# A hybrid decoder layer in fp32 halves: another order of the projections on all five engines

## The chip, the cores and the metric

One core of a Trainium2 chip runs the whole layer as one program. The metric is device time in microseconds (us), the median of several executions. TensorE (PE) does the matmuls, VectorE (DVE), ScalarE (ACT) and GpSimd (POOL) the element work, and SyncE (SP) issues every DMA. Each engine works through its own list in order; they meet only at semaphores.

## The reference, cut to what matters

```
c_act = silu(c);  mod = c_act @ w_ada + b_ada          # sh1, sc1, g1, sh2, sc2, g2: 1024 each
h    = rms_norm(x, norm1_g) * (1 + sc1) + sh1          # x: 2048 x 1024
proj = h @ w_in                                        # 1024 -> 2304: q,k,v | val,gate | bg,cg,xc | ud
ya   = diff_attention(q, k, v)                         # q, k rms-normed per 32 columns, causal
yb   = silu(layer_norm(causal_dwconv31(val * sigmoid(gate)) + b))     # 256 channels
yc   = bg * causal_dwconv3(cg * xc)
yd   = (pooled windows 2,4,8,16 of ud - ud) @ pool_w * pool_scale
x    = x + g1 * (concat(ya, yb, yc, yd) @ w_out)
x    = x + g2 * (relu(rms_norm(x)*(1 + sc2) + sh2 @ w_ff1)^2 @ w_ff2)
```

## The kernel before, in words

The program has three stages: the projections (to about 570 us), the attention (to about 950 us), and w_out with the MLP (the rest). Only the first is touched. Every fp32 operand of a projection is split into a rounded head (`h_hi`, `w_hi`, made on ACT) and a tail (`h_lo`, `w_lo`, made on DVE), and each product is three matmuls (lines L1617 to L1619). A weight item (256 columns) therefore goes SP load -> ACT head (L778) -> DVE tail (L1170), through one raw buffer: the next load waits for the tail.

The tokens come in two halves, h = 0 and 1, of 1024 each. A half has two parts.

*Row tiles*, t = 0 to 7, n = 8h + t. PE transposes a tile of x (`transposes`, L1627) into the first two PSUM banks; ACT applies gain and shift (`modulate`, eight instructions, L794) and makes the head (`h_head`, L800); DVE makes the tail (`h_tail`, L1165); then PE projects q, k and v of the tile. Before it is transposed, x is loaded by SP (`load_x`, two buffers), its mean square is taken by DVE (`mean_square`, L1149 to L1152), the root by ACT (`rms_root`, L785), and the rows are scaled by DVE (`normalise`, L1158 and L1159). In the kernel before, round t of the loops does the mean square, root and scaling of tile n+2 and the modulation, head and tail of tile n+1. q and k are normed by `qk_square`, `qk_sums`, `qk_normalise` (DVE, L1229 to L1239) and by POOL (`norm_gain`), and stored.

*Columns*: kinds gate, val, ud, cg, pool, xc, bg, each with two blocks of 512 tokens times two groups of 128 channels. The outputs go round a ring of six PSUM banks, and `free(o)` makes PE wait for the reader of the output six before. DVE multiplies val by the sigmoid of the gate into `conf` and then runs the 31-tap convolution: 124 instructions per half (`conv_taps`, L1256 and L1259), which other work calls for in portions by `pump(taps, n)`; what is left of them runs into the next half's row tiles, or into the attention. POOL sums the windows of ud (`windows`, L694 to L699) into `win_a` and `win_b`; DVE makes `pool_in` (`pooled`, L1294 to L1303); ACT may overwrite ud's two tiles for the second block only when DVE has saved their end (`halo_saved`). DVE multiplies xc by cg (`in_prod`, L1309), and makes the short convolution and its product with bg (`short`, L1320 to L1325).

Beside this POOL sums the modulation (`modulation`, L715) row by row from weights that SP loads and ACT scales (`scale_ada`, L886); two small PE products per half (`modulation`, L1686) finish it, and DVE reads them (`read_norm_vector`, `read_gate`). In the second half the sum lies in `norm_acc`, at 187.25 KB, where `win_a` and `win_b` lie too, so that POOL's second-half windows begin with

```
                if h:
                    pool.wait_ge(mod2_mm, 3)
```

that is, after the first of the second half's two modulation products on PE. The layer norm of the convolution has two PE sums (`ln_sum`, L1697), with DVE (`ln_sub`, `ln_scale`, L1275 to L1284) and ACT (`ln_square`, `ln_root`, `ln_silu`) between; for half 0 it is done among half 1's work, for half 1's second block in the attention. `LN_AT` says before which kinds the sums stand.

Of the kernel before, what the change touches and what calls it, by code (L numbers as in the profile page):

```python
# [21 lines left out]
P = 128  # L22
# [38 lines left out]
def projections():  # L61


    out = []

    for h in range(2):
        for t in range(0, HT, 2):
            out += [("qk", h, t, 0), ("qk", h, t + 1, 0), ("v", h, t, 0)]
        for kind in ("gate", "val", "ud", "cg", "pool", "xc", "bg"):
            for b in range(NB):  # L70
                if h and kind in LN_AT:
                    out.append(("ln",) + LN_AT[kind] + (b,))
                out += [(kind, h, c, b) for c in range(GC)]
    return out
# [4 lines left out]
LN_AT = {"gate": (0, 0), "val": (0, 1), "bg": (1, 0)}  # L79
# [62 lines left out]
def trunk(nc, x, c, w_ada, b_ada, norm1_g, norm2_g, w_in, w_out, q_norm_g, k_norm_g, lam_params,  # L142
# [3 lines left out]
    with ctx:  # L146
# [52 lines left out]
        pool_in = sb("pool_in", 170.5, [P, GC, HALF])  # L199
# [229 lines left out]
        def _(sp):  # L429
# [68 lines left out]
            def store_mixer(h, chunk, ready):  # L498
                for b in range(NB):
# [23 lines left out]
            for h in range(2):  # L523
                w0 = h * NI
                for t in range(HT):
# [3 lines left out]
                    if n + 2 < NT:  # L529
                        load_x(n + 2)  # L530
# [128 lines left out]
        def _(pool):  # L659
# [59 lines left out]
            for h in range(2):  # L719
# [49 lines left out]
        def _(act):  # L769
# [129 lines left out]
            for h in range(2):  # L899
                w0 = h * NI  # L900
                for t in range(HT):
                    n = h * HT + t
                    if t + 1 < HT:
                        modulate(n + 1, h_tmp, gain1, shift1)
                        h_head(n + 1, h_tmp)
                    if n + 2 < NT:
                        rms_root(n + 2)
# [8 lines left out]
                    if t % 2:  # L916
                        scale_ada(h, t // 2)
                qk_square(h * HT + HT - 1)
                copy_v(h, HT - 2)
                w_in_head(w0 + 4)  # L920
                if h:
                    ln_square(0, 0)
# [4 lines left out]

                def middle():
                    scale_ada(h, 5)
                    if h:  # L930
                        ln_root(0, 0)

                each_block("gate", h, to_gated(ACT.Sigmoid), middle)
                w_in_head(w0 + 6)
                if h:
                    ln_silu(0, 0)
# [10 lines left out]
                each_block("cg", h, to_gated(ACT.Copy))  # L947
                each_block("pool", h, to_pool_stage)
                if h == 0:
                    w_in_head(NI)  # L950
# [183 lines left out]
        def _(dve):  # L1134
# [209 lines left out]

            taps = iter(())
            blocks = [(cc, b) for b in range(NB) for cc in range(GC)]
            for h in range(2):
                w0 = h * NI
                for t in range(HT):
                    n = h * HT + t  # L1350
                    if n + 2 < NT:
                        dve.wait_ge(x_ld[n % 2], 16 * ((n + 2) // 2 + 1))
                        mean_square(n + 2, x_in[n % 2])
                    if t + 1 < HT:
                        h_tail(n + 1, h_tmp)
                    if n + 2 < NT:
                        normalise(n + 2, x_in[n % 2][:, :], x_in[n % 2][:, :])
# [5 lines left out]
                    pump(taps, 4)  # L1363
# [5 lines left out]
                if h:  # L1369
                    ln_sub(0, 0)  # L1370
                w_in_tail(w0 + 5)
                if h:
                    ln_scale(0, 0)
                w_in_tail(w0 + 6)
                if h:
                    ln_sub(0, 1)
                for cc, b in blocks:
# [10 lines left out]
                    if h and (cc, b) == (GC - 1, 0):  # L1388
                        ln_scale(0, 1)
                w_in_tail(w0 + 7)  # L1390
                pump(taps, 16)
                read_norm_vector(h)
                for cc, b in blocks:
                    if (cc, b) == (0, 1):
                        w_in_tail(w0 + 8)
                    pooled(h, cc, b)
                    pump(taps, 4)
                read_gate(h)

                dve.wait_ge(proj_ready, OUT_NO["pool", h, GC - 1, NB - 1] + 1)  # L1400
                link(V.tensor_copy(prod[:, :, 0:STAPS - 1], halo2[:, :, :]))
                for cc, b in blocks:
# [3 lines left out]
                    pump(taps, 7)  # L1406
# [3 lines left out]
                for cc, b in blocks:  # L1410
# [3 lines left out]
                    if h or (cc, b) != blocks[-1]:  # L1414
                        pump(taps, 3)
                    if h and (cc, b) == (GC - 1, 0):
                        ln_scale(1, 0)
                if h == 0:
                    h_tail(HT, h_tmp)
# [190 lines left out]
        def _(pe):  # L1610
# [50 lines left out]
            def project_cols(kind, h, w, middle=lambda: None):  # L1661

                layer_norm(kind, h, 0)
                item_ready(w)
                wh, wl = w8(w, w_hi), w8(w, w_lo)
                for b in range(NB):
                    if b:
                        middle()
                        layer_norm(kind, h, 1)
                    for cc in range(GC):  # L1670
                        o = OUT_NO[kind, h, cc, b]
# [28 lines left out]
            def layer_norm(kind, h, s):  # L1700
                if h and kind in LN_AT:
                    free(OUT_NO[("ln",) + LN_AT[kind] + (s,)])
                    ln_sum(*LN_AT[kind], s).then_inc(proj_ready, 1)
# [7 lines left out]
            def next_tile():  # L1711
                pe.wait_ge(mod2_ready, 1)
                transposes(HT, x_in[HT % 2])

            for h in range(2):
                w0 = h * NI
                for t in range(HT):
                    n = h * HT + t
                    if t + 1 < HT:
                        transposes(n + 1, x_in[(n + 1) % 2])  # L1720
# [16 lines left out]
                for i, kind in enumerate(("gate", "val", "ud", "cg")):  # L1737
                    project_cols(kind, h, w0 + 3 + i, (lambda: modulation(h, 1)) if kind == "cg" else (lambda: None))
                    if kind == "ud":
                        modulation(h, 0)  # L1740
# [201 lines left out]
```

## Time and profile before

| | us |
|---|---|
| median of 3 runs | 2667.37 (2664.5 to 2668.7) |
| span of the profiled execution | 2665.4 |
| PE busy in the span | 2456.0 (92%) |
| DVE busy | 1635.7 (61%) |
| ACT busy | 874.7 (33%) |
| POOL busy | 236.0 (9%) |
| mean granted TensorE clock | 0.957 |

The span runs from the first to the last instruction of the profiled execution; its own time is not given beside it. The median of the runs is 2.0 us above the span. A row of the timeline reads: start, duration, engine, line, operation, tiles written <- read, count, and in brackets the idle time of the engine before it with what ended it.

### The profile page before, as it was taken

Reading aid. Unit: us, or ns where it says so; the run is one execution under the profiler, and the core shown is the slowest. Engines: PE = TensorE matmul, PEld = TensorE weight load, DVE = VectorE, ACT = ScalarE, POOL = GpSimd, SP = SyncE. Lnnn points to the kernel's source line nnn. Section 1 sums busy time; section 2 is a strip of 40 time slices with the busy share of each in tenths; the row PEclk is TensorE's granted clock in tenths of the full one; section 3 lists DMA queues with packets and bytes.
Section 4 is the critical chain, followed back from the end, with each engine's and each line's share of the span. In section 5 each row is a group of like instructions: output and inputs, shape, how many; then the busy total and the mean of one; then the engine's idle time right before and its main releaser. Section 6 shows DMA issues by size and latency. Waiting matters only on the chain.

```text
span 2665.4 us, 31399 instructions
## 1 busy us (share of the span) xinstructions
PE 2456.0 (92%) x11970; PEld 2035.8 (76%) x11970; DVE 1635.7 (61%) x2749; ACT 874.7 (33%) x1365; POOL 236.0 (9%) x145
## 2 busy tenths in 40 slices
PE   6997898875878997989999999999989999999999
PEld 3985796654767775868888888887877888888887
DVE  3649885986788895654555555555655545454544
ACT  3532354135677774432121212122431111212120
POOL 0233042411222200000000000000000000000000
PEclk8998999976799997999999999999999999999999
DMA  6442234110000003211111111114311111111111
GB/s 225 141 129 71 95 120 141 56 68 16 29 13 9 21 9 111 87 64 48 48 47 47 47 47 47 47 47 150 118 48 55 41 63 40 54 47 47 47 47 63
DMA packets 107002, 176.66 MB, mean 66 GB/s; under 512 B 5000, under 2 KB 76956, under 8 KB 105884
## 3 DMA queue, kind: packets, MB, share of 16 engines
q1 hardware_dynamic: 106908, 175.40, 19.8%
q8 instruction: 59, 0.97, 0.2%
q14 instruction: 35, 0.29, 0.0%
HBM read 152.32 MB, written 23.07 MB: 66 GB/s over the span
## 4 chain that ended last, share of the span: by engine, by line
PE 65%; DVE 16%; issue 6%; ACT 6%; DMA 4%; POOL 2%; SPq 1%; POOLq 0%; ACTq 0%; DVEq 0%
PE ps L1617 18%; PE ps L1618 18%; PE ps L1619 18%; DVE sb_acc L1259 5%; PE ps L1876 2%; PE ps L1878 2%; PE ps L1877 2%; ACT sb_scores L991 2%; DVE sb_w_lo L1170 2%; PE ps L1812 2%; DVE sb_scores L1435 1%; DVE sb_scores L1450 1%; POOL sb_gate_row L715 1%; ACT sb_w_hi L778 1%; DMA sb_x_in<-in_x 1%
## 5 line engine op out<-in xcount | busy, mean ns | idle before, releaser
L1617 PE MATMUL ps<-sb_h_hi,sb_w_hi 128*128 128x512 f32 x1408 | 557.4, 396 | 13.1 <-DVE sb_w_lo L1170 11.3
L1618 PE MATMUL ps<-sb_h_lo,sb_w_hi 128*128 128x512 f32 x1408 | 550.3, 391 | 0.0
L1619 PE MATMUL ps<-sb_h_hi,sb_w_lo 128*128 128x512 f32 x1408 | 549.9, 391 | 0.0
L1567 DVE TENSOR_TENSOR sb_x_new<-sb_x_new,ps 128x512 f32<-128x512 f32 x512 | 344.6, 686 | 213.5 <-PE ps L1619 211.4
L1617 PE MATMUL ps<-sb_w_hi,sb_u_hi 128*128 128x512 f32 x1024 | 399.8, 390 | 10.0 <-DVE sb_x_new L1567 10.0
L1618 PE MATMUL ps<-sb_w_lo,sb_u_hi 128*128 128x512 f32 x1024 | 398.9, 390 | 0.0
L1619 PE MATMUL ps<-sb_w_hi,sb_u_lo 128*128 128x512 f32 x1024 | 398.9, 390 | 0.0
L1097 ACT ACTIVATE sb_relu_t<-ps 128x512 f32<-128x512 f32 x128 | 76.1, 594 | 929.1 <-PE ps L1619 868.6
L1617 PEld LDWEIGHTS ps<-sb_h_hi,sb_w_hi 128*128 128x128 f32 x1408 | 266.3, 189 | 73.8 <-DVE sb_w_lo L1170 12.3
L1618 PEld LDWEIGHTS ps<-sb_h_lo,sb_w_hi 128*128 128x128 f32 x1408 | 265.9, 189 | 58.2 <-issue 3.5
L1619 PEld LDWEIGHTS ps<-sb_h_hi,sb_w_lo 128*128 128x128 f32 x1408 | 265.8, 189 | 55.9
L1552 DVE TENSOR_TENSOR sb_relu_t<-sb_relu_t 128x512 f32<-128x512 f32 x128 | 88.7, 693 | 358.0 <-ACT sb_relu_t L1097 358.0
L1170 DVE TENSOR_TENSOR sb_w_lo<-sb_w_raw,sb_w_hi 128x2048 fp32r<-128x2048 f32 x88 | 204.5, 2324 | 102.9 <-ACT sb_w_hi L778 102.9
L1617 PEld LDWEIGHTS ps<-sb_w_hi,sb_u_hi 128*128 128x128 f32 x1024 | 192.6, 188 | 52.5 <-DVE sb_x_new L1567 12.6
L1619 PEld LDWEIGHTS ps<-sb_w_hi,sb_u_lo 128*128 128x128 f32 x1024 | 192.5, 188 | 40.1
L1618 PEld LDWEIGHTS ps<-sb_w_lo,sb_u_hi 128*128 128x128 f32 x1024 | 192.6, 188 | 39.9
L778 ACT ACTIVATE sb_w_hi<-sb_w_raw 128x2048 fp32r<-128x2048 f32 x88 | 168.2, 1911 | 155.5 <-DVE sb_w_raw L1178 68.4
L1259 DVE SCALAR_TENSOR_TENSOR sb_acc<-sb_conf,sb_col,sb_acc 128x512 f32<-128x512 f32 x240 | 206.3, 925 | 0.2
L1435 DVE TENSOR_SCALAR_CACHE_REDUCE sb_scores<-ps 128x512 f32<-128x512 f32 (+3 forms) x320 | 179.3, 607 | 42.7 <-PE ps L1792 22.1
L1822 PE MATMUL ps<-sb_v_sb,sb_a_t 128*128 128x64 f32 x1088 | 154.8, 291 | 31.0 <-ACT sb_a_t L1002 21.5
L1822 PEld LDWEIGHTS ps<-sb_v_sb,sb_a_t 128*128 128x128 f32 x1088 | 143.6, 206 | 39.4 <-ACT sb_a_t L1002 28.5
L991 ACT ACTIVATE sb_scores<-sb_scores,sb_bst 128x128 f32<-128x128 f32 (+15 forms) x128 | 152.4, 1198 | 0.1
(187 smaller groups left out, 3147.5 us busy)
## 6 DMA issues: line engine op xcount, KB each, us to landing
sb_w_raw<-in_w_ff SPq DMA_DIRECT2D x64, 1024.0 KB, 5.1
sb_w_raw<-in_w_in SPq DMA_DIRECT2D x18, 1024.0 KB, 5.9
sb_ada<-in_w_ada SPq DMA_DIRECT2D x32, 512.0 KB, 4.8
sb_ada_first<-in_w_ada SPq DMA_DIRECT2D x8, 1024.0 KB, 7.6
sb_x_in<-in_x SPq DMA_DIRECT2D x16, 512.0 KB, 5.6
sb_x_new<-in_x SPq DMA_DIRECT2D x16, 512.0 KB, 4.8
out<-sb_x_new SPq DMA_DIRECT2D x16, 512.0 KB, 4.7
sb_mix_in<-mix_scratch SPq DMA_DIRECT2D x14, 512.0 KB, 4.1
```

Of the source, the lines that this page charges most:

```text
L778: A(w_hi[s][:, :], raw[:, :], ACT.Copy).then_inc(whi_ready, 1)
L991: A(prob(u, m, 0, n), prob(u, m, 0, n), ACT.Exp, scale=SCALE, bias=bst[:, s, 10 + m:11 + m], accum_out=bst[:, s, 12 + m:13 + m]).then_inc( ...
L1097: A(relu_t[f][:, :], psum[:, 2 + f % 2, :], ACT.Relu).then_inc(relu_ready, 1)
L1170: V.tensor_tensor(out=w_lo[s][:, :], in0=raw[:, :], in1=f32(w_hi[s][:, :]), op=ALU.subtract).then_inc(wlo_ready, 1)
L1259: ins = V.scalar_tensor_tensor(out=dst, in0=src, scalar=w, in1=dst, op0=ALU.mult, op1=ALU.add)
L1435: V.tensor_scalar(prob(u, m, c0, n), psum[:, r % 4, 0:n], 1.0, None, ALU.mult, ALU.max, accum_out=bst[:, s, 4 * m + ch:4 * m + ch + 1]).th ...
L1552: V.tensor_tensor(out=relu_t[f][:, :], in0=relu_t[f][:, :], in1=relu_t[f][:, :], op=ALU.mult).then_inc(sq_ready, 1)
L1567: V.tensor_tensor(out=y, in0=y, in1=psum[:, 4 + o % 4, :], op=ALU.add).then_inc(ff2_read, 1)
L1617: M(dst, ah, bh, start=(n == 0), stop=False)
L1618: M(dst, ah, bl, start=False, stop=False)
L1619: ins = M(dst, al, bh, start=False, stop=(n == last))
L1822: ins = M(psum[:, 6, 0:VD], a_t[gn % 2][:, k * P:(k + 1) * P], v_sb[:, k0 + k, hd * VD:(hd + 1) * VD], start=(k0 + k == 0), stop=(k0 + k = ...
```

## The change

On PE, the transposes of the second half run two tiles ahead instead of one, the first two of its tiles are transposed between the last blocks of the first half's bg, the layer-norm sums of block 0 stand before row tiles 2 and 4, those of block 1 before the second blocks of gate and val; the two modulation products stand after cg and after xc instead of after ud and within cg; the pooled products stand after xc instead of before it. ACT and DVE follow: roots and scaling now stand before the modulation and the tail in both halves, and `pump` portions are dealt out anew. `pool_in` moves to its own place, so that it no longer shares one with `prod`.

```
@@ projections()
             for t in range(0, HT, 2):
+            if h and t in LN_ROWS:
+                out.append(("ln",) + LN_ROWS[t])
-        for kind in ("gate", "val", "ud", "cg", "pool", "xc", "bg"):
+        for kind in ("gate", "val", "ud", "cg", "xc", "pool", "bg"):
-LN_AT = {"gate": (0, 0), "val": (0, 1), "bg": (1, 0)}
+LN_ROWS = {2: (0, 0, 0), 4: (0, 0, 1)}
+LN_COLS = {("gate", 1): (0, 1, 0), ("val", 1): (0, 1, 1), ("bg", 0): (1, 0, 0), ("bg", 1): (1, 0, 1)}
-        pool_in = sb("pool_in", 170.5, [P, GC, HALF])
+        pool_in = sb("pool_in", 199.75, [P, GC, HALF])
@@ sync
-                    if n + 2 < NT:
-                        load_x(n + 2)
+                    if n + 2 + h < NT:
+                        load_x(n + 2 + h)
                 if h == 0:
                     load_w_in(NI + 1)
+                    load_x(HT + 2)
@@ gpsimd
                 modulation(h, 4)
-                modulation(h, 5)
                 if h:
                     ln_out(0, 0)
+                modulation(h, 5)
@@ scalar, row tiles
-                    if t + 1 < HT:
-                        modulate(n + 1, h_tmp, gain1, shift1)
-                        h_head(n + 1, h_tmp)
-                    if n + 2 < NT:
-                        rms_root(n + 2)
+                    if n + 2 + h < NT:
+                        rms_root(n + 2 + h)
+                    if t + 1 + h < HT:
+                        modulate(n + 1 + h, h_tmp, gain1, shift1)
+                        h_head(n + 1 + h, h_tmp)
+                    (second half: ln_square(0, 0) at t == 2, ln_root(0, 0) at t == 4)
@@ scalar, end of the first half
-                    modulate(HT, h_tmp, gain1, shift1)
-                    act.wait_ge(*used(NI - 1))
-                    h_head(HT, h_tmp)
+                    for n in (HT, HT + 1):
+                        modulate(n, h_tmp, gain1, shift1)
+                        if n == HT:
+                            act.wait_ge(proj_ready, OUT_NO["bg", 0, GC - 1, 0] + 1)
+                        h_head(n, h_tmp)
+                        if n == HT:
+                            rms_root(HT + 2)
@@ vector, row tiles
-                    mean_square(n + 2); if t + 1 < HT: h_tail(n + 1, h_tmp); normalise(n + 2)
+                    load_squares(n + 2 + h); scale_rows(n + 2 + h)
+                    if t + 1 + h < HT:
+                        h_tail(n + 1 + h, h_tmp)
+                    (second half: ln_sub(0, 0) at t == 2, ln_scale(0, 0) in place of pump at t == 5)
@@ vector, columns
                 w_in_tail(w0 + 7)
-                pump(taps, 16)
-                read_norm_vector(h)
                 for cc, b in blocks:
                     if (cc, b) == (0, 1):
                         w_in_tail(w0 + 8)
+                    pump(taps, 6)
                     pooled(h, cc, b)
-                    pump(taps, 4)
-                read_gate(h)
+                pump(taps, 8)
+                read_norm_vector(h)
                 for cc, b in blocks:
                     in_prod(h, cc, b)
-                    pump(taps, 7)
+                    pump(taps, 8)
+                read_gate(h)
                 for cc, b in blocks:
                     short(h, cc, b)
-                    if h or (cc, b) != blocks[-1]:
+                    if h or b == 0:
                         pump(taps, 3)
+                    if h == 0 and (cc, b) == (GC - 1, 0):
+                        h_tail(HT, h_tmp)
+                        load_squares(HT + 2)
+                    if h == 0 and (cc, b) == (0, 1):
+                        h_tail(HT + 1, h_tmp)
+                        scale_rows(HT + 2)
@@ tensor
-                    if t + 1 < HT:
-                        transposes(n + 1, x_in[(n + 1) % 2])
+                    if t + 1 + h < HT:
+                        transposes(n + 1 + h, x_in[(n + 1 + h) % 2])
+                    if h and t in LN_ROWS:
+                        layer_norm(*LN_ROWS[t])
                 for i, kind in enumerate(("gate", "val", "ud", "cg")):
-                    project_cols(kind, h, w0 + 3 + i, (lambda: modulation(h, 1)) if kind == "cg" else ...)
-                    if kind == "ud":
-                        modulation(h, 0)
+                    project_cols(kind, h, w0 + 3 + i)
+                modulation(h, 0)
+                project_cols("xc", h, w0 + 7)
+                modulation(h, 1)
                 (the pooled products)
-                project_cols("xc", h, w0 + 7)
-                project_cols("bg", h, w0 + 8, (lambda: None) if h else next_tile)
+                project_cols("bg", h, w0 + 8, {} if h else {
+                    (0, 1): lambda: next_tile(HT), (1, 1): lambda: next_tile(HT + 1)})
```

## Rows read from the trace of the kernel before

**Rows 1.** Busy time by stretch: us, busy per engine with instructions, PEclk, DMA share, GB/s.
```profile
184.00:313.00 129.00, 109.12 (x471) 86.08 (x470) 114.49 (x143) 27.57 (x39) 29.86 (x17) 0.92 0.27 86
445.00:581.00 136.00, 118.51 (x486) 91.56 (x487) 121.52 (x145) 33.90 (x43) 43.78 (x25) 0.94 0.21 69
```
**Rows 2.** The waits between 184 and 620 us: us in total, times, longest.
```profile
POOL sb_win_a L694 <- issue: 9.6, 1, 9.6
PE ps L1748 <- DVE sb_pool_in L1298: 17.8, 4, 6.7
```
**Rows 3.** Timeline of DVE, row tiles of the first half: start, us, instruction, idle before.
```profile
114.54 0.70 DVE L1149 BATCH_NORM_STATS2 sb_bn<-sb_x_in 128x6 f32<-128x512 f32 x1 [3.69 <-DMA sb_x_in<-in_x]
116.11 0.22 DVE L1152 SCALAR_TENSOR_TENSOR sb_stat<-sb_stat 128x1 f32<-128x1 f32 x1
121.75 2.41 DVE L1152 SCALAR_TENSOR_TENSOR sb_stat<-sb_stat 128x1 f32<-128x1 f32 x1
```
**Rows 4.** Timeline of ACT beside it.
```profile
121.25 2.88 ACT L794 ACTIVATE sb_h_tmp<-ps,sb_shift,sb_gain 128x128 f32<-128x128 f32 x8
124.16 1.06 ACT L800 ACTIVATE sb_h_hi<-sb_h_tmp 128x1024 fp32r<-128x1024 f32 x1
125.13 0.28 ACT L785 ACTIVATE sb_stat<-sb_stat,sb_small 128x1 f32<-128x1 f32 x1
```
**Rows 5.** Timeline of DVE, the second half's row tiles.
```profile
319.35 2.73 DVE L1259 SCALAR_TENSOR_TENSOR sb_acc<-sb_conf,sb_col,sb_acc 128x512 f32<-128x512 f32 x4
...
336.78 1.23 DVE L1165 TENSOR_TENSOR sb_h_lo<-sb_h_tmp,sb_h_hi 128x1024 fp32r<-128x1024 f32 x1 [3.75 <-ACT sb_h_hi L800]
338.79 0.68 DVE L1229 TENSOR_REDUCE sb_small<-sb_qk_sq 128x16 f32<-128x512 f32 x1
340.13 0.69 DVE L1239 TENSOR_TENSOR sb_qkv_out<-ps,sb_small 128x512 f32<-128x512 f32 x1
340.74 3.69 DVE L1259 SCALAR_TENSOR_TENSOR sb_acc<-sb_conf,sb_col,sb_acc 128x512 f32<-128x512 f32 x4
```
**Rows 6.** Timeline of DVE, from one half to the other.
```profile
313.19 0.69 DVE L1149 BATCH_NORM_STATS2 sb_bn<-sb_x_in 128x6 f32<-128x512 f32 x1 [8.00 <-DMA sb_x_in<-in_x]
```
**Rows 7.** Timeline of SP, the loads that open the second half.
```profile
304.43 0.38 SPq L455 DMA_DIRECT2D sb_w_raw<-in_w_in  x1
```
**Rows 8.** Timeline of PE: tile 9, gate, gate's and val's second blocks, modulation product.
```profile
318.64 0.56 PE L1617 MATMUL ps<-sb_w_hi,sb_h_hi 128*128 128x256 f32 x1
396.28 0.80 PE L1617 MATMUL ps<-sb_h_hi,sb_w_hi 128*128 128x512 f32 x1
420.60 0.94 PE L1617 MATMUL ps<-sb_h_hi,sb_w_hi 128*128 128x512 f32 x1
447.92 0.79 PE L1617 MATMUL ps<-sb_h_hi,sb_w_hi 128*128 128x512 f32 x1
481.01 1.88 PE L1686 MATMUL ps<-sb_norm_acc,sb_ones_mean 128*128 128x512 f32 x4
```
**Rows 9.** Timeline of DVE, the convolution's end in the second half.
```profile
409.45 2.29 DVE L1170 TENSOR_TENSOR sb_w_lo<-sb_w_raw,sb_w_hi 128x2048 fp32r<-128x2048 f32 x1 [13.45 <-ACT sb_w_hi L778]
```
**Rows 10.** Timeline of POOL, the second half's windows.
```profile
483.02 6.64 POOL L694 TENSOR_TENSOR sb_win_a<-sb_ud 128x527 f32<-128x527 f32 x1 [9.63 <-issue]
500.90 1.06 POOL L694 TENSOR_TENSOR sb_win_a<-sb_ud 128x527 f32<-128x527 f32 x1 [2.12 <-DVE sb_pool_in L1298]
502.05 1.39 POOL L695 TENSOR_TENSOR sb_win_b<-sb_win_a 128x525 f32<-128x525 f32 x1
```
**Rows 11.** Timeline of DVE, pooled inputs to the first scores.
```profile
491.45 0.73 DVE L1298 SCALAR_TENSOR_TENSOR sb_pool_in<-sb_win_a,sb_inv_win,sb_ud 64x512 f32<-64x512 f32 x1
524.97 0.69 DVE L1309 TENSOR_TENSOR sb_prod<-ps,sb_gated 128x512 f32<-128x512 f32 x1 [4.19 <-issue]
561.03 0.68 DVE L1284 TENSOR_TENSOR sb_acc<-sb_acc,sb_ln_rs 128x512 f32<-128x512 f32 x1
580.39 0.29 DVE L1435 TENSOR_SCALAR_CACHE_REDUCE sb_scores<-ps 128x128 f32<-128x128 f32 x1 [5.50 <-PE ps L1792]
```

More of the change, by code:

```diff
@@ L496, in store_v, with store_mixer @@
                              qkv_out[s][:, :].rearrange("p (t d) -> p t d", t=2)).then_inc(qkv_st[s], 16)
-            def store_mixer(h, chunk, ready):
-                for b in range(NB):
+            def store_mixer(h, chunk, ready, blocks=range(NB)):
+                for b in blocks:
                     for cc in range(GC):
@@ L917, in _ @@
                         scale_ada(h, t // 2)
+                    if h and t == 2:
+                        ln_square(0, 0)
+                    if h and t == 4:
+                        ln_root(0, 0)
                 qk_square(h * HT + HT - 1)
@@ L926, in _ @@
                     act.wait_ge(prod_ready, NB * GC * h)
[L928 to L933, printed above, removed]
+                    ln_silu(0, 0)
+                each_block("gate", h, to_gated(ACT.Sigmoid), lambda: scale_ada(h, 5))
                 w_in_head(w0 + 6)
                 if h:
-                    ln_silu(0, 0)
                     ln_square(0, 1)
@@ L1362, in _ @@
                         w_in_tail(w0 + 2)
-                    pump(taps, 4)
+                    if h and t == 2:
+                        ln_sub(0, 0)
+                    if h and t == 5:
+                        ln_scale(0, 0)
+                    else:
+                        pump(taps, 4)
                 w_in_tail(w0 + 3)
@@ L1368, in _ @@
                 pump(taps, 9 * TAPS)
-                if h:
-                    ln_sub(0, 0)
                 w_in_tail(w0 + 5)
                 if h:
-                    ln_scale(0, 0)
+                    ln_sub(0, 1)
                 w_in_tail(w0 + 6)
-                if h:
-                    ln_sub(0, 1)
                 for cc, b in blocks:
@@ L1387, in _ @@
                         pump(taps, 6)
-                    if h and (cc, b) == (GC - 1, 0):
+                    if h and (cc, b) == (0, 1):
                         ln_scale(0, 1)
                 w_in_tail(w0 + 7)
-                pump(taps, 16)
-                read_norm_vector(h)
+                for q in range(2):
+                    dve.wait_ge(qkv_st[q], 16 * (h + 1) * (HT + HT // 2) // 2)
                 for cc, b in blocks:
@@ L1395, in _ @@
                         w_in_tail(w0 + 8)
+                    pump(taps, 6)
                     pooled(h, cc, b)
-                    pump(taps, 4)
-                read_gate(h)
-                dve.wait_ge(proj_ready, OUT_NO["pool", h, GC - 1, NB - 1] + 1)
+                pump(taps, 8)
+                read_norm_vector(h)
+                if h:
+                    dve.wait_ge(lnout_ready, NB * GC)
                 link(V.tensor_copy(prod[:, :, 0:STAPS - 1], halo2[:, :, :]))
@@ L1666, in project_cols @@
                 for b in range(NB):
-                    if b:
-                        middle()
-                        layer_norm(kind, h, 1)
+                    if h and (kind, b) in LN_COLS:
+                        layer_norm(*LN_COLS[kind, b])
                     for cc in range(GC):
+                        if (cc, b) in before:
+                            before[cc, b]()
                         o = OUT_NO[kind, h, cc, b]
@@ L1698, in ln_sum, with layer_norm @@
                 return ins
[L1700 to L1703, printed above, removed]
+            def layer_norm(h, b, s):
+                free(OUT_NO["ln", h, b, s])
+                ln_sum(h, b, s).then_inc(proj_ready, 1)
             def project_v(h, t):
@@ L1709, in project_v, with next_tile @@
                 return project_rows(h, t, h * NI + 2, bank(o)[:, t % 2 * GW:(t % 2 + 1) * GW])
-            def next_tile():
+            def next_tile(n):
                 pe.wait_ge(mod2_ready, 1)
-                transposes(HT, x_in[HT % 2])
+                transposes(n, x_in[n % 2])
             for h in range(2):
```

29 lines of the change are left out of this document (13 added, 16 removed).

## The prediction

> **What bounds the kernel now.** I read the busy time by stretch first. In both halves' columns PE is not the only full engine: DVE is busy for 114.5 of 129.0 us and for 121.5 of 136.0 [rows 1], since the convolution's 248 instructions lie there. Then the waits: PE stands still for DVE's pooled inputs (17.8 us in four waits), and POOL waits once for 9.6 us for something that is no engine's work in the list [rows 2]; the timelines say what it is: PE's modulation product runs from 481.01 to 482.89 [rows 8], and the first window sum of the second half starts at 483.02 [rows 10]. That is the semaphore quoted above. Last the timelines of the joints: DVE waits 8.0 us for x between the halves [rows 6] and 13.45 us for a weight head in the second half's gate [rows 9].
>
> So the change takes PE's visible idle time (pooled products, the joint of the halves) as what it moves, while DVE, in order, sets when half of this stage ends. I follow four clocks through it: tile 9, the gate, the end of cg, DVE's first pooled input; all shifts are against the rows.
>
> **Row tiles, first half.** Before, round t let the mean square of tile n+2 (114.54 to 116.33, 1.8 us [rows 3]) run beside the modulation of tile n+1 on ACT (2.88, then the head 1.06 [rows 4]). Now ACT has the root first, so the modulation waits for the mean square. The round becomes one chain: mean square 1.8, root 0.3 [rows 4], modulation 2.9, head 1.1, tail 1.2, q and k norm 2.0 (338.79 to 340.82) [rows 5] = 9.3 us, against a PE tile of 9.5 (tile 9 to the gate is 77.6 us for seven tiles [rows 8], with some 6 of idle time and a sum of 1.9 in it, and one tile without v). That alone would just fit. But every second round POOL's modulation sum catches the last step of the mean square (2.41 instead of 0.22 [rows 3]) and so now the modulation, and twice x lands late (the 3.69 us wait at 114.54 [rows 3]) with the modulation now behind it. Walking the eight rounds: tile 1 is 1.9 us later (x of tile 2 must land first), tile 6 waits 1.3, tile 7 waits 5.4 and then starts slowly, as tile 9 did after its wait (its first matmul took 0.56 us [rows 8]); 1.8 us for that is my estimate. PE reaches the gate about 7.6 us late, and the ACT, POOL and SP chain behind it 6.2 us late. Bounds: 0 (if the chain hides in PE's lead) and 10.
>
> **Columns, first half, and the joint.** From w_lo of xc on, DVE never rests, so its own sum counts. It starts 6.2 late; it gains the 4.2 us wait that stood at in_prod (the second half's is 4.19 [rows 11]) and some 1.7 of POOL contention; it takes on the scaling of tile 10 and the tail of tile 9 (1.8 + 1.0 + 1.2 = 4.0), one more convolution step (0.7), about 2.6 us of waiting for bg's weight head (the tail now stands right behind the second pooled input, which frees ACT to make the head: 0.6 + 1.9 of ACT), and 1.5 for the head of tile 9. DVE ends at 305.2 (313.19 less 8.00 [rows 6]) + 9.1 = 314.3. Then SP: x of tile 11 is queued behind the four stores of the short convolution, as x of tile 10 was, and behind a weight load; from that load's issue to x it took 8.8 us (304.43 to 313.19 [rows 6, 7]). So x arrives at 323.5, PE's transposes of tile 11 wait for the modulation of tile 10 behind its root, and tile 9 starts at about 330.1, 11.5 us later than 318.64 [rows 8]. The idle time at this joint is not removed; it moves one tile on. Bounds: 0 and 16.
>
> **Row tiles, second half.** The lead of two tiles gives slack, but the transposes of tile n+2 stand ahead of tile n on PE and wait for the modulation of n+1, which waits for the mean square of n+2 on DVE, behind a pump. Chain per round: 9.3 as above plus four convolution steps, 2.73 alone or 3.69 beside POOL [rows 5], and about 2.2 more beside a POOL sum. So 12.9, 12.8, 14.2 (with ln_sub 1.4), 15.0, 13.5, 11.8 (ln_scale instead of the pump), 5.7, 5.7 and the weight tail 2.3 = 93.9 us from x's arrival to the gate: 417.4, against 396.28 [rows 8], +21.1. Before, DVE idled only where ACT's head was late (3.75 once [rows 5]); now it idles some 3 us in each of five rounds between scaling and tail. Bounds for this step: 0 (PE's pace holds) to +15; I take 9.6, as the chain of DVE and ACT in order leaves no way round.
>
> **The gate.** Its first block now needs no sum, but the sums before its second need the whole convolution of block 1: eight steps (5.4 us) behind the tail of val's weights. That tail started 13.2 us after the gate before [rows 8, 9] and the second block 24.3 after the first. The chain ACT head, POOL sum, SP load, 8 us, head, tail is the same; 5.4 us of steps stand where 3.4 of steps, a subtraction and a square stood. Second block at 441.8, +21.2: nothing gained.
>
> **Val, ud, cg.** Six blocks ran from 447.92 to 481.01 [rows 8], 5.5 us each; four of cg more would have ended at 503.2. Now one sum and a 1.7 us wait less: 441.8 + 79.3 = 521.1, +17.9.
>
> **The windows, which decide it.** PE's first modulation product of the second half now stands behind cg, four blocks or 22.1 us later in PE's order, and POOL's second-half windows wait for it. They could start at 523.0; the first takes 2.5 (1.06 + 1.39 [rows 10]); DVE makes its first pooled input at 525.5, against 491.45 [rows 11]: +34.1. DVE is then long there (six steps after xc's weight tail, near 495) and in order: convolution steps queue behind the wait and can't fill it. ACT's ud of the second block, bg's weight head and the cg copies hang behind it too. If DVE reached it later, the stall would shrink, but not the clock 525.5, which is PE's.
>
> **From there to the attention.** Before, 491.45 to 561.71 at the end of ln_scale [rows 11]. Now 14 more convolution steps (64 for 50) lie in it, 9.5 us, with read_norm_vector 2.8 and the wait for bg's head 2.6; the 4.7 of waiting at in_prod and 1.7 of contention go: +8.5. From ln_scale to the first scores the chain over ACT, POOL and the transposes is as before (18.7). Four steps fewer wait in the attention: -2.7. PE's own waits here (bg behind in_prod, for the ring) are hidden by DVE.
>
> **Sum.** 34.1 + 8.5 - 2.7 = 39.9 us on the profiled execution's 2665.4. Its time is given by the span alone; the median lies 2.0 above it, so 2667.4 + 39.9 = 2707 us.
>
> **A rule weighed.** POOL's first window sum took 6.64 us beside DVE's back-to-back steps and 1.06 beside an idle DVE [rows 10]. In the sum the windows meet a waiting DVE, hence 2.5. The Trainium skill, in SBUF — State Buffer, section "SBUF: two separate sides", says that the port pair DVE and GpSimd share is an exclusive lock, held for a whole instruction. By that rule 2.5 is right too; without it, at 6.64, the sum would be 5.6 higher, 2713.
>
> **Rivals.** (a) *Rows keep PE's pace.* For it: the lead of two tiles, and rounds of 9.3 us in the first half. Against: the chain runs through one ACT list. Then the first half's 6.2, the second's 9.6 go; cg ends near 505.2, the first pooled input is at 509.6, +18.2; with 8.5 - 2.7 the sum is +24: 2691 us. Chance 0.25. (b) *Everything prepared early works.* The joint's idle time (8.0) and the 6.6 us around tile 15 go as well; cg ends at 487 or before, which is the point from which the windows no longer stall DVE beyond 491.45. What stays is at most the later convolution steps: +5 or less, 2664 to 2672 us; below 0 if PE's gains also reach DVE. For it: x of tiles 8 to 10 is there early. Against: SP's stores before x of tile 11. Chance 0.09. (c) *More contention.* The portions fall beside POOL's sums oftener, or a stall cools PE's clock in each tile: the row steps at their upper bounds (3 + 5) and windows against taps (5): about 2720 us. Chance 0.16. My forecast has 0.50.
>
> **Range.** 2684 to 2722 us: it takes in (a) and (c) and leaves (b). About 0.2%, 5 us, can be told from no change. Faster 0.05, same 0.05 (both from b, with a little for what I have not seen), slower 0.90.
>
> **What would show it.** Right: L694 of the second half begins just behind L1686 near 523 us; DVE's wait before its first L1298 there is 20 us or more with the releaser POOL; in the row tiles each group of L794 starts behind an L785 and DVE idles 3 us before each L1165; tile 9 starts near 330, the gate near 417. Wrong: PE reaches the end of cg before 500, DVE arrives at L1298 without a wait, or the wait is there and the end of ln_scale is not shifted.

## The result and the profile after

The changed kernel takes 2704.91 us (median of 4 runs, 2701.26 to 2707.88), the kernel before 2668.03 us beside it (4 runs, 2664.50 to 2669.33): ratio 1.0138, 95% interval 1.0123 to 1.0152. It is slower by 1.4%, 36.9 us. The profiled executions have spans of 2700.9 and 2665.4 us, 35.5 apart. DVE is as busy as before (1634.6 us in the span, against 1635.7). PE is busy 11.0 us longer (2467.0 against 2456.0) with the same 11970 matmuls, at a mean granted clock of 0.951 against 0.957. No engine got more work; what was added is waiting, and on PE some time at the lower clock.

By stretch, the columns of the first half up to the x that opens the second, and the second half from val's second block to the first scores (to set beside [rows 1]; us, then busy us per engine with instructions):

```profile
190.50:324.50 134.00, 110.44 (x480) 88.11 (x478) 117.26 (x151) 28.08 (x40) 29.69 (x17) 0.92 0.28 90
466.00:622.00 156.00, 124.55 (x481) 93.99 (x479) 120.41 (x146) 32.14 (x42) 39.30 (x24) 0.86 0.17 57
```

The first stretch grew from 129 to 134 us, the second from 136 to 156, and in the second DVE's busy time hardly changed (121.5 before, 120.4 now) and its idle time went from 14.5 to 35.6 us. The waits of 184 to 660 us (us in total, times, longest; beside [rows 2]) say on what:

```profile
POOL sb_win_a L698 <- issue: 24.5, 1, 24.5
...
DVE sb_pool_in L1303 <- POOL sb_win_b L699: 22.8, 1, 22.8
...
DVE sb_h_lo L1170 <- ACT sb_h_hi L804: 16.5, 7, 2.9
...
DVE sb_bn L1154 <- DMA sb_x_in<-in_x: 9.6, 1, 9.6
```

The first two are one wait, POOL's for a semaphore and DVE's for POOL. PE no longer waits for the pooled inputs; that part of the change did what it says, and bought nothing that can be seen, since DVE, which makes them, is the one that is late.

PE's timeline at the same places as [rows 8]: tile 7, the transposes of tile 11, tile 9, the gate, its second block, and the modulation product.

```profile
135.25 0.58 PE L1635 MATMUL ps<-sb_w_hi,sb_h_hi 128*128 128x256 f32 x1 [5.29 <-DVE sb_h_lo L1170]
...
329.57 1.94 PE L1645 MATMUL ps<-sb_ident,sb_x_in 128*128 128x128 f32 x8 [8.54 <-ACT sb_h_tmp L798]
...
331.16 0.56 PE L1635 MATMUL ps<-sb_w_hi,sb_h_hi 128*128 128x256 f32 x1
...
417.65 0.80 PE L1635 MATMUL ps<-sb_h_hi,sb_w_hi 128*128 128x512 f32 x1 [5.58 <-DVE sb_w_lo L1175]
...
440.99 1.42 PE L1635 MATMUL ps<-sb_h_hi,sb_w_hi 128*128 128x512 f32 x1
...
520.21 1.88 PE L1704 MATMUL ps<-sb_norm_acc,sb_ones_mean 128*128 128x512 f32 x4
```

ACT in a row tile of the second half: root, modulation, head (beside [rows 4], where the modulation came first):

```profile
339.02 0.29 ACT L789 ACTIVATE sb_stat<-sb_stat,sb_small 128x1 f32<-128x1 f32 x1 [6.71 <-DVE sb_stat L1157]
339.23 2.88 ACT L798 ACTIVATE sb_h_tmp<-ps,sb_shift,sb_gain 128x128 f32<-128x128 f32 x8
342.14 1.06 ACT L804 ACTIVATE sb_h_hi<-sb_h_tmp 128x1024 fp32r<-128x1024 f32 x1
```

DVE beside it: x of tile 11, one round's scaling and tail, and the tail of val's weights (beside [rows 5, 6, 9]):

```profile
324.53 0.69 DVE L1154 BATCH_NORM_STATS2 sb_bn<-sb_x_in 128x6 f32<-128x512 f32 x1 [9.56 <-DMA sb_x_in<-in_x]
...
339.35 0.16 DVE L1163 RECIPROCAL sb_stat<-sb_stat 128x1 f32<-128x1 f32 x1 [0.36 <-ACT sb_stat L789]
...
343.23 1.23 DVE L1170 TENSOR_TENSOR sb_h_lo<-sb_h_tmp,sb_h_hi 128x1024 fp32r<-128x1024 f32 x1 [2.93 <-ACT sb_h_hi L804]
...
430.49 2.29 DVE L1175 TENSOR_TENSOR sb_w_lo<-sb_w_raw,sb_w_hi 128x2048 fp32r<-128x2048 f32 x1 [10.94 <-ACT sb_w_hi L782]
```

POOL's first windows of the second half, and DVE from there to the first scores (beside [rows 10, 11]):

```profile
522.23 1.06 POOL L698 TENSOR_TENSOR sb_win_a<-sb_ud 128x527 f32<-128x527 f32 x1 [24.45 <-issue]
523.37 1.06 POOL L699 TENSOR_TENSOR sb_win_b<-sb_win_a 128x525 f32<-128x525 f32 x1
```

```profile
524.46 0.74 DVE L1303 SCALAR_TENSOR_TENSOR sb_pool_in<-sb_win_a,sb_inv_win,sb_ud 64x512 f32<-64x512 f32 x1 [22.83 <-POOL sb_win_b L699]
...
601.93 0.68 DVE L1289 TENSOR_TENSOR sb_acc<-sb_acc,sb_ln_rs 128x512 f32<-128x512 f32 x1
...
621.74 0.29 DVE L1453 TENSOR_SCALAR_CACHE_REDUCE sb_scores<-ps 128x128 f32<-128x128 f32 x1 [5.96 <-PE ps L1812]
```

Read as shifts against the rows of before, the loss is built in four steps: tile 9 is 12.5 us late (331.16 against 318.64), the gate 21.4 (417.65 against 396.28), the first pooled input 33.0 (524.46 against 491.45), the first scores 41.4 (621.74 against 580.39). After that nothing is added; at the first output of the stage behind the attention the shift is 35.9 (1089.01 against 1053.11).

### The profile page after: what moved, and what is told of

Same layout as the page of the kernel before. It is cut to its first block, busy times and chain, and to the rows that moved or that the text cites. A ratio compares the mean times of both kernels' runs of the same rounds, so it can differ in the third digit from the quotient of the medians.

```text
span 2700.9 us, 31398 instructions
## 1 busy us (share of the span) xinstructions
PE 2467.0 (91%) x11970; PEld 2042.2 (76%) x11970; DVE 1634.6 (61%) x2749; ACT 871.0 (32%) x1363; POOL 231.2 (9%) x145
## 4 chain that ended last, share of the span: by engine, by line
PE 63%; DVE 16%; issue 7%; ACT 7%; DMA 4%; POOL 2%; SPq 0%; POOLq 0%; ACTq 0%; DVEq 0%
PE ps L1635 18%; PE ps L1636 18%; PE ps L1637 17%; DVE sb_acc L1264 5%; PE ps L1898 2%; PE ps L1896 2%; PE ps L1897 2%; ACT sb_scores L996 2%; DVE sb_scores L1453 2%; DVE sb_scores L1468 2%; DVE sb_w_lo L1175 2%; PE ps L1832 1%; ACT sb_h_tmp L798 1%; ACT sb_w_hi L782 1%; POOL sb_gate_row L719 1%
## 5 line engine op out<-in xcount | busy, mean ns | idle before, releaser
L1635 PE MATMUL ps<-sb_h_hi,sb_w_hi 128*128 128x512 f32 x1408 | 557.6, 396 | 29.6 <-DVE sb_w_lo L1175 14.5
L1453 DVE TENSOR_SCALAR_CACHE_REDUCE sb_scores<-ps 128x512 f32<-128x512 f32 (+3 forms) x320 | 179.1, 606 | 40.7 <-PE ps L1812 21.4
L1264 DVE SCALAR_TENSOR_TENSOR sb_acc<-sb_conf,sb_col,sb_acc 128x512 f32<-128x512 f32 x240 | 200.7, 900 | 0.2
L1842 PE MATMUL ps<-sb_v_sb,sb_a_t 128*128 128x64 f32 x1088 | 153.6, 290 | 31.0 <-ACT sb_a_t L1007 21.4
```

Of the source, the lines that this page charges most:

```text
L1264: ins = V.scalar_tensor_tensor(out=dst, in0=src, scalar=w, in1=dst, op0=ALU.mult, op1=ALU.add)
L1453: V.tensor_scalar(prob(u, m, c0, n), psum[:, r % 4, 0:n], 1.0, None, ALU.mult, ALU.max, accum_out=bst[:, s, 4 * m + ch:4 * m + ch + 1]).th ...
L1635: M(dst, ah, bh, start=(n == 0), stop=False)
L1842: ins = M(psum[:, 6, 0:VD], a_t[gn % 2][:, k * P:(k + 1) * P], v_sb[:, k0 + k, hd * VD:(hd + 1) * VD], start=(k0 + k == 0), stop=(k0 + k = ...
```

## The experiments

Each kernel was measured beside the kernel before; its ratio is to that. The median of the kernel before was 2668.03, 2662.19, 2669.13 and 2663.24 us in the four comparisons, so medians of different comparisons aren't compared, only ratios; one thousandth is 2.7 us.

**1. The modulation product back behind ud, in the second half alone** (e1).

```
@@ tensor
                 for i, kind in enumerate(("gate", "val", "ud", "cg")):
                     project_cols(kind, h, w0 + 3 + i)
-                modulation(h, 0)
+                    if h and kind == "ud":
+                        modulation(h, 0)
+                if h == 0:
+                    modulation(h, 0)
```

> The changed kernel with one thing put back: in the second half PE's first modulation product stands after ud again, so that POOL's windows may start some 22 us earlier. Theory (the windows' wait is what the time is lost to, DVE in order behind it): the first window sum starts near 500 us, DVE's first pooled input near 502 instead of 524.5, its wait there falls from 22.8 us to about 1, and nearly all of it reaches the end: 2705 - 22 = 2683 us, ratio to before 1.0055. Rival (the row tiles' chain or DVE's added steps cost it, the wait is only where it shows): DVE then waits for PE at the next joint (in_prod or bg), under 8 us come back: 2697 us or more.

Measured: 2682.54 us, ratio 1.0078 (1.0056 to 1.0100), 0.0060 or 16 us below the changed kernel's. From the two intervals I estimate 9 to 23 us for this difference; the expected 22 lies at its upper end, and the profiled executions are 22.7 apart (2678.2 against 2700.9). In the trace POOL and DVE:

```profile
498.31 1.35 POOL L698 TENSOR_TENSOR sb_win_a<-sb_ud 128x527 f32<-128x527 f32 x1 [2.78 <-issue]
```

```profile
501.16 0.75 DVE L1303 SCALAR_TENSOR_TENSOR sb_pool_in<-sb_win_a,sb_inv_win,sb_ud 64x512 f32<-64x512 f32 x1 [0.95 <-POOL sb_win_b L699]
```

The 22.83 us wait is gone, and the first pooled input is 23.3 us earlier, with nothing else in the kernel changed. So it is the place of one PE product of 1.88 us that costs them, through a semaphore that POOL waits for.

**2. The old order of root and modulation, scaling and tail** (e2): the rest of the change stays, the late product too.

```
@@ scalar, row tiles
-                    if n + 2 + h < NT:
-                        rms_root(n + 2 + h)
                     if t + 1 + h < HT:
                         modulate(n + 1 + h, h_tmp, gain1, shift1)
                         h_head(n + 1 + h, h_tmp)
+                    if n + 2 + h < NT:
+                        rms_root(n + 2 + h)
@@ vector, row tiles: likewise h_tail(n + 1 + h) ahead of scale_rows(n + 2 + h)
```

> The changed kernel with the order of root, modulation, scaling and tail in the row tiles as before (modulation and head ahead of the root on ACT, tail ahead of the scaling on DVE), the lead of two tiles kept, and the modulation product after cg kept. Theory (the chain mean square - root - modulation - head - tail sets the rounds): DVE's 2.9 us wait in each round goes, the second half's gate starts near 400 us instead of 417.7, all after it moves with PE, 2705 - 17 = 2688 us. Rival (the rounds are DVE's own work, 12 to 15 us with the convolution steps, or POOL contention): the gate at 412 or later, 2700 us.

Measured: 2681.62 us, ratio 1.0077 (1.0054 to 1.0100). PE at the gate, DVE at the first pooled input:

```profile
396.77 0.80 PE L1636 MATMUL ps<-sb_h_hi,sb_w_hi 128*128 128x512 f32 x1 [4.12 <-DVE sb_w_lo L1175]
```

```profile
503.94 0.74 DVE L1303 SCALAR_TENSOR_TENSOR sb_pool_in<-sb_win_a,sb_inv_win,sb_ud 64x512 f32<-64x512 f32 x1 [23.09 <-POOL sb_win_b L699]
```

The gate is back at 396.8, where it was before the change (396.28); in e3 below, which is the same up to there, it came at 400.9. So 17 to 21 of the 21.4 us at the gate come from the order in the row tiles, somewhat more than the 15.8 us (6.2 + 9.6) I gave it. The 4.2 us between these two executions, which run the same work up to there, are also how far a single shift can be trusted. The windows' wait stays as long as it was (23.09), so it does not come from the row tiles.

**3. Both** (e3: the edits of 1 and 2).

> Both put back: modulation product of the second half after ud, and the old order within the row tiles. Theory (two separate losses in a row on one path, and together all of the loss): they add, 2705 - 22 - 17 = 2666 us, no difference from before (ratio 0.998 to 1.002). Rival (both hide the same time): 2680 us, with DVE's wait at the pooled input still 10 us or more or moved to in_prod.

Measured: 2663.46 us, ratio 1.0000 (0.9983 to 1.0017). The two edits account for the whole loss. By the first pooled input they add nearly in full: e1 brings it 23.3 us forward, e2 20.5, both 37.8, that is 6.0 less than the sum, of which 4.2 is the difference between the executions of e2 and e3 at the gate. What is left of the change (earlier layer norm, tiles prepared at the end of the first half, pooled products later) is worth nothing in sum. DVE still waits 9.97 us at the joint for x of tile 11, and its first pooled input stands at 486.70, 4.8 us before the old kernel's; by the end of `ln_scale` that lead has become a lag of 3.2, a shift of 7.9 where I had +8.5.

**4 and 5. Each cause put into the kernel before** (b2: both second-half products behind cg; b1: the new order of root, scaling, modulation and tail, in both halves).

```
@@ b2, tensor
-                    project_cols(kind, h, w0 + 3 + i, (lambda: modulation(h, 1)) if kind == "cg" else (lambda: None))
-                    if kind == "ud":
+                    project_cols(kind, h, w0 + 3 + i,
+                                 (lambda: modulation(0, 1)) if kind == "cg" and h == 0 else (lambda: None))
+                    if kind == ("cg" if h else "ud"):
                         modulation(h, 0)
+                if h:
+                    modulation(1, 1)
```

> The kernel before with one thing of the change: in the second half PE's two modulation products stand after cg. Theory (the windows' wait is a price by itself, whatever the rows do): the first window sum moves from 483.0 to about 505 us, DVE's first pooled input from 491.5 to about 508, and the difference stays to the end: +16.5 us, ratio 1.006. Rival (it costs only behind the slower row tiles, since PE's cg is then late): under 4 us, ratio below 1.0015.

> The kernel before with one thing of the change: in the row tiles the root stands ahead of the modulation on ACT and the scaling ahead of the tail on DVE, with the lead of one tile as before. Theory (mean square, root, modulation, head and tail become one chain per round): the first half's last weight tail before conf is some 7 us later, each round of the second half has 3 us of DVE waiting, and with one tile of lead PE waits for it in each: +20 us, 2688 us, ratio 1.0075 (more than 1.005). Rival (PE's and DVE's slack takes it): +6 us or less.

Measured: b2 2681.73 us, ratio 1.0048 (1.0035 to 1.0061), 12.8 us; b1 2691.67 us, ratio 1.0079 (1.0059 to 1.0099), 21 us. Both are slower, as theory had it. In b2 POOL starts the windows here, 20.2 us later than in [rows 10], but DVE makes the first pooled input only 14.4 us later than in [rows 11]. POOL, then DVE:

```profile
503.19 1.06 POOL L694 TENSOR_TENSOR sb_win_a<-sb_ud 128x527 f32<-128x527 f32 x1 [31.38 <-issue]
```

```profile
503.09 1.23 DVE L1185 TENSOR_TENSOR sb_h_tmp<-ps,sb_ident 128x1024 f32<-128x1024 f32 x1 [15.93 <-PE ps L1686]
...
505.88 0.73 DVE L1298 SCALAR_TENSOR_TENSOR sb_pool_in<-sb_win_a,sb_inv_win,sb_ud 64x512 f32<-64x512 f32 x1
```

DVE's wait is not one for POOL. L1185 is `read_norm_vector`, which waits for the same modulation product by the same semaphore, and in the kernel before and in b2 it stands ahead of the pooled inputs; it takes 2.8 us, and the windows are done meanwhile (505.39). In the kernel before DVE came to it late, from its own convolution steps, and did not wait at all:

```profile
478.06 10.68 DVE L1259 SCALAR_TENSOR_TENSOR sb_acc<-sb_conf,sb_col,sb_acc 128x512 f32<-128x512 f32 x16
488.65 1.22 DVE L1185 TENSOR_TENSOR sb_h_tmp<-ps,sb_ident 128x1024 f32<-128x1024 f32 x1
```

The product ended at 482.89 there, 5.8 us before DVE asked for it, and that slack is what came back of the 20.2 us; the first window's 6.64 us against 1.06 here changed nothing, since both sums were done at 490.80, before DVE pooled. So b2 shows that the late product costs the kernel before too, but through DVE's own wait for it. That it costs through POOL's windows, as in the changed kernel, where `read_norm_vector` stands behind the pooled inputs, rests on e1 and the rows there. Counted from the gate, at which this execution was 1.8 us ahead (394.5 against 396.28), the first pooled input is 16.2 us later, the expected 16.5; in the times it is 12.8, with an interval of 9 to 16. In b1 six rounds of the second half show the wait before the tail, 2.93 us each, and the gate comes at 421.73, even later than in the changed kernel: the lead of two tiles recovers about 4 of some 25 us.

**6. The old order in the first half only** (e5).

> The changed kernel with the old order in the row tiles of the first half alone. It splits the 23 us that the old order in both halves gave back. Theory, from the two traces: the first half's chain makes 7.3 us of it (the weight tail ahead of conf at 190.2 and 182 us), so 2705 - 7 = 2698 us, ratio 1.011; the rest, 14 to 16 us, belongs to the second half's rounds. Rival (DVE has slack in the first half's columns and the joint takes up the rest): under 3 us.

Measured: 2694.96 us, ratio 1.0094 (1.0074 to 1.0115), 12 us below the changed kernel's; the expected 1.011 lies within the interval. By the trace the gate is at 410.50, 7.2 us earlier than in the changed kernel, and 9.6 and 13.7 later than in e3 and e2. So the first half's rounds cost about 7 us and the second half's 10 to 14, where the prediction had 6.2 and 9.6.

**7 and 8. x of tile 11 asked for before the short convolution's stores** (e4 on e3; e8 on the changed kernel itself).

```
@@ sync
-                    if n + 2 + h < NT:
+                    if n + 2 + h < NT and n != HT:
                         load_x(n + 2 + h)
...
-                store_mixer(h, 4, short_ready)
+                store_mixer(h, 4, short_ready, range(1))
+                if h == 0:
+                    load_x(HT + 3)
+                store_mixer(h, 4, short_ready, range(1, NB))
```

> As the kernel with both put back, and SP loads x of tile 11 after the first two stores of the short convolution instead of after all four and a weight load. Theory (the joint's idle time stands on that load): x of tile 11 lands near 305 us, DVE's wait of 9.6 us between the halves goes, tile 9 starts 8 to 10 us earlier: 2657 us, ratio 0.996, faster than both kernels. Rival (the joint is DVE's work, scaling of tile 10 behind the short convolution): less than 3 us, 2664 us.

> The changed kernel with one edit, SP's load of x of tile 11 after the first two stores of the short convolution. Theory (the joint's wait was moved one tile on and stands on SP's order): the 9.6 us wait of DVE goes, PE's transposes of tile 11 start near 321 instead of 329.6 us and everything behind them moves: 2705 - 8 = 2697 us, ratio 1.0105. Rival (the rounds behind it are the bound, and DVE's work at the joint fills the gap): 3 us or less, ratio above 1.0125.

Measured: e4 2655.62 us, ratio 0.9967 (0.9955 to 0.9979), faster than the kernel before and, against e3's 1.0000, by 9 us; e8 2697.37 us, ratio 1.0133 (1.0111 to 1.0156), which can't be told from the changed kernel's 1.0138 and fits the rival's expectation. The traces say that the edit did its work in both. In e8 DVE's 9.56 us wait is gone and PE reaches the gate 8.9 us sooner:

```profile
408.76 0.80 PE L1638 MATMUL ps<-sb_h_hi,sb_w_hi 128*128 128x512 f32 x1 [5.64 <-DVE sb_w_lo L1178]
```

and the first scores start at 612.05, 9.7 us sooner than in the changed kernel. Yet the stage behind the attention starts at nearly the same time in both (1089.3, and 1089.7 in the changed kernel): the profiled execution of e8 lost the gain in the attention, where no instruction differs. That stretch in the changed kernel, in e3, e4 and e8, in this order (the column behind the busy times is the granted clock):

```profile
684.30:1089.00 404.70, 336.12 (x2233) 285.73 (x2234) 324.74 (x990) 284.40 (x470) 73.55 (x35) 0.91 0.10 32
```

```profile
648.30:1052.40 404.10, 332.27 (x2233) 281.89 (x2234) 324.92 (x991) 284.48 (x470) 73.56 (x35) 0.92 0.10 33
```

```profile
636.50:1047.20 410.70, 339.33 (x2233) 288.91 (x2234) 327.27 (x990) 284.86 (x470) 72.70 (x35) 0.90 0.10 31
```

```profile
677.00:1088.50 411.50, 338.57 (x2233) 288.25 (x2234) 327.42 (x991) 284.69 (x470) 72.73 (x35) 0.90 0.10 32
```

404 us at a granted clock of 0.91 to 0.92, 411 at 0.90. Over the twelve traces it lies between 403.7 (0.93) and 411.5 (0.90); e7 below has the early load too and 405.2 us at 0.91, so the load isn't shown to cause it. What sets the clock of that stretch stays open. Whether the early load is worth 8 us in the changed kernel's time is not settled either: up to the attention it gives 9.7, in the times nothing that can be told.

**9. The convolution's last steps ahead of the tail of val's weights** (e6, on e4).

```
@@ vector, columns
-                w_in_tail(w0 + 4)
                 pump(taps, 9 * TAPS)
+                w_in_tail(w0 + 4)
```

> The kernel with both put back and the early load of x of tile 11, and on DVE the rest of the first half's convolution steps ahead of the weight tail of val instead of behind it. Theory (PE stands 6.7 us before the second block of gate for eight steps that wait in order behind a tail whose head is not there, while DVE idles 10.8 us): PE's wait goes, with the slow start behind it 8 us, the columns of the second half all move by that: 2655.6 - 8 = 2648 us, ratio 0.9935. Rival (the next joint, the sums before val's second block or the layer norm's store, takes it up): 3 us or less, 2653 us.

Measured: 2658.65 us, ratio 0.9959 (0.9946 to 0.9972), not to be told from e4's 0.9967; the rival was right. PE's wait of 6.66 us before the sums at the gate's second block went, and two others came in its place, at sums before val's second block and at the modulation product:

```profile
432.17 3.75 PE L1719 MATMUL ps<-sb_ln_sq,sb_ones_mean 128*128 128x512 f32 x4 [3.58 <-ACT sb_ln_sq L844]
...
472.52 3.78 PE L1708 MATMUL ps<-sb_norm_acc,sb_ones_mean 128*128 128x512 f32 x4 [3.12 <-POOL sb_norm_acc L722]
```

DVE waits longer too where it opens the next convolution, for the store of the layer norm, 5.44 us against 1.66 in e4. So freeing PE at one joint is not enough here. By the longest waits left (13.6 us of DVE for a weight head, 9.4 of ACT for a weight) it is the weights' way over SP, ACT and DVE that ends this stretch, but no run separates that.

**10. bg's weight tail behind the convolution's portion** (e7, on e6): `pump(taps, 6)` before `w_in_tail(w0 + 8)` in the pooled loop.

> The kernel with all the edits so far (old row order, modulation product after ud, early x of tile 11, convolution's rest ahead of val's weight tail), and bg's weight tail on DVE behind the six convolution steps of its round instead of ahead of them. Theory (DVE waits 2.53 us in each half for bg's head, which ACT can only make after the second pooled input, while steps lie ready behind it): both waits go, each worth its time since DVE is full on either side: 2658.6 - 5 = 2654 us, ratio 0.994. Rival (the steps then run beside POOL's windows and lose the time to contention): 2658 us, no gain.

Measured: 2651.37 us, ratio 0.9958 (0.9944 to 0.9973): no gain over e6 that can be told, against 5 us expected. DVE's 2.53 us wait before that tail is gone, but from the first pooled input to the first scores only 0.9 us of it is left (96.4 against 97.3). The rival's reason is what the trace shows: the six steps, which in e6 ran behind POOL's window sums, now run beside them and take 1.70 us longer. In e6, then in e7:

```profile
494.28 4.06 DVE L1267 SCALAR_TENSOR_TENSOR sb_acc<-sb_conf,sb_col,sb_acc 128x512 f32<-128x512 f32 x6
```

```profile
485.44 5.76 DVE L1267 SCALAR_TENSOR_TENSOR sb_acc<-sb_conf,sb_col,sb_acc 128x512 f32<-128x512 f32 x6
```

e4, e6 and e7 beat both kernels, at about 0.996.

## Why the prediction was right

The forecast was 2707 us, measured were 2704.91; sign, place and cause hold. By its steps:

- **First half's row tiles** (PE 7.6 late at the gate, the weight chain 6.2). Right: tile 7 waits 5.29 for the forecast 5.4 and starts with matmuls of 0.41 us, the first half's gate is 6.8 us late (148.52 against 141.75), the last weight tail 6.5. The slow start I put at 1.8 us: the first 17 matmuls took 3.80 us instead of 2.04 (17 of 0.12), 1.8 us.
- **The joint** (DVE ends at 314.3, x at 323.5, tile 9 at 330.1). Measured 314.97 (324.53 less 9.56), 324.53 and 331.16. The idle time moved one tile on, as said: PE waits 8.54 us for the modulation of tile 10 behind its root.
- **Second half's row tiles** (gate at 417.4). 417.65. The five waits of 3 us before the tail are there, 2.93 each, and each modulation stands behind a root. I gave the order 15.8 us of the 21.1 and the joint the rest; e2 and e3 give the order 17 to 21, so that it was sized low by 1 to 5 us and the rest high by as much.
- **The gate, and val to cg** (second block 441.8, cg's end 521.1). 440.99 and 520.21, 0.9 early; nothing gained there, PE waits 7.21 us before the sums for the convolution's last step.
- **The windows** (start 523.0, first pooled input 525.5, DVE's wait 20 us or more). 522.23, 524.46, 22.83, with POOL the releaser. e1 shows the cause. In the kernel before the windows held nobody up: DVE's first pooled input at 491.45 stood behind its own steps and `read_norm_vector`. The forecast of 34.1 needs only that row and PE's new clock, so it holds; but a late product costs that kernel through another wait, as b2 shows.
- **The rule weighed.** The windows took 1.06 us each beside a waiting DVE, so the 2.5 us of the sum hold (2.23 from POOL's start to DVE's), not 6.64. One row was misread, though: the window at 500.90, which I gave as beside an idle DVE, had convolution steps beside it. It took 1.06 us all the same, and DVE paid, 4.43 us for four steps instead of 2.73 [rows 5]:

```profile
500.88 4.43 DVE L1259 SCALAR_TENSOR_TENSOR sb_acc<-sb_conf,sb_col,sb_acc 128x512 f32<-128x512 f32 x4
```

The Trainium skill, SBUF — State Buffer, section "SBUF: two separate sides", says that of a GpSimd instruction that reads SBUF and a DVE instruction with two SBUF inputs, as these steps have, whichever starts first has the pair for its whole instruction and the other is blocked. The traces agree that the one or the other pays. That POOL's sum at 483.02 was held over eight of DVE's steps (6.64 us) is more than one instruction, and this sentence does not foretell it.
- **To the end of `ln_scale`** (+8.5) **and in the attention** (-2.7). The shift grew from 33.0 to 40.9 (602.61 against 561.71), by 7.9; at the end of the second block's `ln_scale` it is 38.7 (684.27 against 645.60), 2.2 less.
- **The sum.** 39.9 forecast; 38.7 at the last point that the change touches, 35.5 at the end of the profiled execution, 36.9 in the medians. The last 3 us need not be the change's: the attention took 2.8 us less in this execution (404.7 against 407.5), which is within what e3 and e8 show for the same instructions.

Of the rivals, (a) fails since the rounds don't keep PE's pace; (b) since x of tile 11 was still late (9.56 us) and cg ended at 520, not 487; (c) wasn't needed, DVE's busy time in the second stretch did not grow (120.4 us against 121.5). What was lucky is that single errors of 1 us had both signs, and that the order's share at the gate, sized 1 to 5 us low, and the rest, high by as much, cancel there; what was sound is that the four clocks were followed separately, so that the two causes add: e1 and e2 take away 16 us each by the times, e3 with both 37. The 4 us between 32 and 37 are within the intervals.

## What to carry to other kernels

Before moving a small instruction later on an engine that has slack, look for what waits on its semaphore: here a 1.88 us product moved by 22 us on PE held POOL, POOL held DVE, and DVE was the engine that ended the stage. List every wait on it, and what is ahead of each: in b2 another wait on the same semaphore, DVE's own, was the one that cost. In a loop over tiles that several engines share, keep what belongs to the tile in hand (modulation, tail) ahead of what prepares the next but one (root, scaling) on each in-order engine; turned round, two short chains become one long chain per round. To find which part of a reordering costs, undo the parts one by one and together: here what was left was worth nothing in sum. One load moved ahead of two stores in SP's queue then gave 9 us on e3; on the changed kernel itself the times show nothing of it.

## What the runs showed of the hardware

A POOL window sum of 128x527 (L694 of the kernel before) took 1.06 us when DVE stood still beside it, and mostly also when DVE ran convolution steps; then DVE paid (6.27 us for four steps from 493.07 in the kernel before, 2.73 alone). Where POOL came into a running stream of steps it went either way. In the kernel before the sum took 6.64 us and ended 0.92 us after the last of sixteen steps, which kept their pace (10.68 us in all); b1 repeats it with 6.66. In e1 a sum that came into such a stream took 1.35 us, and the six steps 7.00 us instead of 4.06, part of it beside an earlier sum. What decides which engine gives way is open.

PE stood idle for 5.29 us before 135.25 in the changed kernel, and the granted clock was down to 0.72 on average over the five us before. After the restart it was 0.50, the lower of the two levels, for four us, and then the upper one:

```profile
130.00:135.00 5.00, 0.00 (x0) 0.00 (x0) 3.46 (x3) 4.39 (x11) 2.02 (x1) 0.72 0.37 97
135.00:139.00 4.00, 3.75 (x17) 3.75 (x18) 2.35 (x5) 0.79 (x2) 1.42 (x2) 0.50 0.67 271
139.00:141.00 2.00, 2.00 (x19) 2.00 (x18) 1.53 (x6) 0.78 (x2) 0.00 (x0) 0.99 0.72 253
141.00:146.00 5.00, 5.00 (x44) 5.00 (x43) 3.06 (x5) 3.28 (x4) 1.44 (x2) 1.00 0.05 18
```

And the attention, with the same instructions in all twelve kernels, varied by 7.8 us between executions with a granted clock between 0.90 and 0.93, more than several of the edits above are worth; single spans can't rank them.
